# Products of ones in front of waits, and wider moving operands, in a two-layer transformer kernel

## The reference, cut to what matters

```python
def first_block(x, ...):            # attention of three kinds, gated branches
    hn = rms_norm(x, ln_g)
    proj = hn @ w_in                # 1024 x 11520
    # q, k, v, silu gates of: block attention (8 heads), dilated attention (3 x 8 heads),
    # sliding window attention with sinks (8 heads), and sigmoid gates
    merged = sum(sigmoid(gate_i) * ((o_i * silu(g_i)) @ w_branch[i]) for i in range(3))
    return x + merged @ w_out

def hybrid_layer(x, c, ...):
    ada = silu(c) @ w_ada + b_ada   # 1024 x 6144, one row: shifts, scales, gates
    h = rms_norm(x) * (1 + scale1) + shift1
    proj = h @ w_in                 # conv part, q, k, v, index q (512), index k and weights (72 columns)
    # indexed attention: top 64 keys for each query by a relu score, then softmax
    x = x + gate1 * (concat(conv_out, attn_out) @ w_out)
    h2 = rms_norm(x) * (1 + scale2) + shift2
    return x + gate2 * moe(h2, ...) # 64 experts, top 8 of each token, and a shared expert
```

## Time and profile before

| | before |
|---|---|
| median of 3 runs | 1109.86 us (1106.12 to 1110.11) |
| profiled execution | 1112.14 us, span of its instructions 1110.3 us |
| TensorE busy (MATMUL) | 1021.8 us, 92% of the span |
| VectorE, ScalarE, GpSimd busy | 796.2, 585.9, 218.9 us |
| mean granted TensorE clock | 0.950 |
| HBM read | 244.27 MB, 222 GB/s over the span |

### The profile page before, as it was taken

One profiled execution on the slowest core, in us unless ns is written; L12 is line 12 of the kernel. 1 busy time (PEld: TensorE's weight loads), 2 busy tenths in 40 slices (PEclk: granted clock), 3 DMA queues, 4 the chain that ended last, 5 costly groups with the idle time before them and its releaser, 6 DMA issues. The chain is left out here.

```text
span 1110.3 us, 16071 instructions
## 1 busy us (share of the span) xinstructions
PE 1021.8 (92%) x4922; PEld 815.6 (73%) x4922; DVE 796.2 (72%) x1324; ACT 585.9 (53%) x895; POOL 218.9 (20%) x237
## 2 busy tenths in 40 slices
PE   5999999997999998979879697999999999999994
PEld 4878877786766675767668576677888788888883
DVE  4677787676654452556686644789999999999995
ACT  4555555334324432334435331677777777778772
POOL 4032220001000000041140000324324233232330
PEclk9999999997999798988899798999999999999997
DMA  9677676747634224434234213878888888888882
GB/s 321 234 261 247 237 235 227 236 162 235 223 107 171 91 96 170 152 93 157 100 128 152 77 40 116 334 292 334 332 313 343 311 325 340 304 345 331 318 345 79
DMA packets 91204, 247.36 MB, mean 223 GB/s; under 512 B 13244, under 2 KB 23925, under 8 KB 77842
## 3 DMA queue, kind: packets, MB, share of 16 engines
q1 hardware_dynamic: 84578, 226.36, 57.0%
q0 software_dynamic: 6000, 19.96, 4.8%
q10 hardware_dynamic: 576, 0.41, 0.1%
HBM read 244.27 MB, written 2.29 MB: 222 GB/s over the span
## 5 line engine op out<-in xcount | busy, mean ns | idle before, releaser
L1746 PE MATMUL bank<-w_hi,a_hi 128*128 128x512 f32 (+2 forms) x512 | 213.9, 418 | 13.8 <-DVE w_lo L1224 7.1
L1746 PE MATMUL bank<-w_lo,a_hi 128*128 128x512 f32 (+2 forms) x512 | 204.6, 400 | 0.0
L1746 PE MATMUL bank<-w_hi,a_lo 128*128 128x512 f32 (+2 forms) x512 | 204.4, 399 | 0.0
L1224 DVE TENSOR_TENSOR w_lo<-ring,w_hi 128x1024 fp32r<-128x1024 f32 (+2 forms) x134 | 154.4, 1177 | 55.0 <-ACT w_hi L947 51.3
L947 ACT ACTIVATE w_hi<-ring 128x1024 fp32r<-128x1024 f32 (+2 forms) x140 | 141.3, 1024 | 97.9 <-PE bank L1746 94.5
L1614 DVE TENSOR_TENSOR up_lo<-raw_weights,up_hi 128x1024 fp32r<-128x1024 f32 x136 | 164.2, 1247 | 3.0
L1107 ACT ACTIVATE up_hi<-raw_weights 128x1024 fp32r<-128x1024 f32 x136 | 135.8, 1050 | 0.0
L1746 PEld LDWEIGHTS bank<-w_hi,a_hi 128*128 128x128 f32 x512 | 101.9, 199 | 45.7 <-issue 23.2
L793 POOL TENSOR_SCALAR mean_squares<-mean_squares 128x8 f32<-128x8 f32 (+2 forms) x32 | 9.9, 310 | 566.7 <-ACT logits L900 301.8
L1746 PEld LDWEIGHTS bank<-w_hi,a_lo 128*128 128x128 f32 x512 | 101.7, 199 | 21.3
L1746 PEld LDWEIGHTS bank<-w_lo,a_hi 128*128 128x128 f32 x512 | 102.0, 199 | 19.8 <-issue 1.4
(11 more groups left out here) (258 smaller groups left out, 1839.2 us busy)
## 6 DMA issues: line engine op xcount, KB each, us to landing
raw_weights<-in_w_dram SPq DMA_DIRECT2D x102, 1024.0 KB, 7.0
ring<-in_w_in_dram SPq DMA_DIRECT2D x58, 1024.0 KB, 5.3
merged<-in_w_ada_dram SPq DMA_DIRECT2D x96, 256.0 KB, 5.3
ring<-in_w_out_dram SPq DMA_DIRECT2D x8, 1024.0 KB, 5.4
ring<-in_w_branch_dram SPq DMA_DIRECT2D x6, 1024.0 KB, 5.0
bias<-rel_rows SPq DMA_DIRECT2D x40, 128.0 KB, 5.2
block_rows<-place_rows SPq DMA_DIRECT2D x34, 128.0 KB, 8.6
ring<-in_ws_dram SPq DMA_DIRECT2D x2, 1024.0 KB, 4.9
```

Of the source, the lines that this page charges most:

```text
L1224: dve.tensor_tensor(w_parts[1][:, 2 * p:2 * p + 2, 0:w], view(JOB[it[1:3]], kind)[:, 2 * p:2 * p + 2, :], w_parts[0][:, 2 * p:2 * p + 2, 0 ...
L1746: mm = pe.matmul(ps[:, 0:w], a_parts[za][:, k, t * P:(t + 1) * P], w_parts[zw][:, k, 0:w], start=start, stop=stop)
```

## The change

A table KEEP_BUSY gives, for 18 places, a number of products of the 128x128 matrix of ones with itself. `keep_busy` issues them on TensorE in front of the wait of that place, into a bank that is overwritten later. The sixteen at the start run before the wait for the constants. In `ada_out` the eight one-column sums move 64 columns of ones (64 equal columns), and VectorE reads one of each 64. Products of the 72-column chunk move 192 columns; the columns above 72 hold older values and are not read. Two waits (for `probsT` and for `valued`) stand earlier in TensorE's queue than before.

```diff
+KEEP_BUSY = {("start",): 16, ("half", "proj", 2, 0): 9, ("proj", 2, 0): 4, ("flip", 15, 2): 5,
+             ("turn_branch", 2): 6, ("xturn", 1, 0): 4, ("xturn", 1, 1): 15, ("proj2", 0, 0): 4, ("turn2", 0, 3, 0): 7,
+             ("turn2", 1): 10, ("value", 31): 8, ("turn_branch", 3, 1): 17, ("out2", 0, 0): 4, ("route", 0): 4,
+             ("route", 1): 5, ("ranks",): 7, ("tokens", 0): 5, ("last_put",): 22}
...
-                        dve.scalar_tensor_tensor(out=mod[rows, m, :], in0=turn_b[rows, 0:KT], scalar=float(s in (1, 4)),
+                        dve.scalar_tensor_tensor(out=mod[rows, m, :], in0=turn_b[rows, 0:CH:HD], scalar=float(s in (1, 4)),
...
+            begun = 0
+
+            def keep_busy(it, ps=None):
+
+                count = KEEP_BUSY.get(it, 0)
+                if count and ps is None:
+                    ps = use_bank(begun)
+                for _ in range(count):
+                    pe.matmul(ps[:, 0:P], ones[:, :], ones[:, :], start=True, stop=True)
+
             for it in SCHEDULE:
                 kind0 = it[0]
                 if kind0 == "start":
+                    pe.wait_ge(S("ones_set"), 2)
+                    keep_busy(it)
                     pe.wait_ge(S("consts_loaded"), 16)
-                    pe.wait_ge(S("ones_set"), 2)
+                elif kind0 != "route":
+                    keep_busy(it)
...
                     ps = use_bank(n) if begins else proj_b[n % 2]
+                    begun = n + 1
...
-                                    mm = pe.matmul(ps[:, 0:w], a_parts[za][:, k, t * P:(t + 1) * P],
-                                                   w_parts[zw][:, k, 0:w], start=start, stop=stop)
+                                    wide = max(w, 3 * HD)
+                                    mm = pe.matmul(ps[:, 0:wide], a_parts[za][:, k, t * P:(t + 1) * P],
+                                                   w_parts[zw][:, k, 0:wide], start=start, stop=stop)
...
                     for t in range(NT):
+                        keep_busy(it + (t,))
                         turn_bank(TURN[it + (t,)])
...
+                            keep_busy(it + (g, t))
                             wide_bank(TURN[it + (g, t)], 2 * z + t)
...
-                            mm = pe.matmul(turn_b[HD * hf:HD * hf + HD, k:k + 1], acc[:, k:CH:KT], ones[:, 0:1],
+                            mm = pe.matmul(turn_b[HD * hf:HD * hf + HD, HD * k:HD * k + HD], acc[:, k:CH:KT], ones[:, 0:HD],
                                            start=True, stop=True)
...
                         pe.wait_ge(S("probs"), 2 * i + 2)
+                        keep_busy(it + (g,))
...
                 if kind0 == "route":
                     t = it[1]
+                    pe.wait_ge(S("probsT"), len(UNITS))
+                    keep_busy(it, flip_b[1])
...
             job_ready(pe, j)
-            pe.wait_ge(S("probsT"), len(UNITS))
...
+            pe.wait_ge(S("valued"), 64)
+            keep_busy(("ranks",), flip_b[1])
             pe.wait_ge(S("taken_ready"), 2)
-            pe.wait_ge(S("valued"), 64)
...
             pe.wait_ge(S("shared_h_0"), 1)
+            keep_busy(("tokens", 0), hidden_b)
             find_tokens(0, 0)
...
                     with pe.If(n_work > i):
                         expert_block(i, (b + 1) % BODY, m4 + 1 + (b + 2) // BODY)
+            keep_busy(("last_put",), turned_b)
             pe.wait_ge(S("put_ready"), n_work)
```

## The result

| | before | changed |
|---|---|---|
| median (4 runs each, taken side by side) | 1107.99 us (1105.23 to 1110.11) | 1094.99 us (1091.53 to 1097.53) |
| profiled execution | 1112.1 us | 1096.3 us, span 1094.5 |
| TensorE busy | 1021.8 us | 1032.3 us |
| mean granted TensorE clock | 0.950 | 0.978 |

The ratio is 0.9873, with a 95% interval of 0.9839 to 0.9907: faster by 10 to 18 us. The forecast was 1094, from 1082 to 1106. The medians differ by 13.0 us, the two profiled executions by 15.8, because the one of the kernel before lies 4.2 above its median and the one of the changed kernel 1.3 above its own.

What follows compares the result with a forecast made beforehand. TensorE, busy 92% of the span, was taken to set the pace. Gains of 25.3 us less 5.6 at the end and 3.7 for growing waits left 16; from 1112.1, less 2.3 to the median, 1094, range 1082 to 1106.

Steps and rivals of the forecast that it cites:

- a: Start of the kernel: products of ones fill the first waits and raise the clock level early; gain 3.3 us.
- b: Sums of the ada products widened to 64 columns: four lower-level stretches behind them vanish; gain 6.4 us.
- i: Stretch at 623.9, heads 30 and 31 to out2: eight products cost, seventeen fit a wait; gain 1.1 us.
- m: Twenty-two products behind the expert loop, before the last scatter: nothing hides them; loss taken as 5.6 us.
- c: Stretch at 507.8, beginning inside the 72-column products: widening to 192 columns gains 3.2 of up to 4.0 us.
- d: Stretch at 367.9: five products in a wait of 1.51 us in front; gain 3.0 us, half the ceiling.
- e: Stretch at 429.3: six products in a wait of 2.24 us, two unfilled waits following; gain 1.8 us.
- j: Router: four and five products of ones; sixteen router products go from 3.67 to 1.9 us; gain 1.8 us.
- g: Stretch at 531.7, index products with waits between: seven products in turn2; gain 1.3 us.
- All hold: Rival: all fills hold and every lower-level stretch but that at 262.1 goes; 1085 us, chance 12%.
- Hidden anyway: Rival: DMA, ScalarE and VectorE pace the front part, so half the gain passes; 1103 us, chance 12%.
- Fills hold only in part: Rival: fills and wide operands hold the level partly, so stretches move rather than vanish; 1104 us, chance 10%.

Runs made afterwards that it cites:

- five executions: First profile and two unedited repeats of the changed kernel (1098.14, 1096.05 us), plus its versions with none (1090.10) and eleven (1091.04) products behind the expert loop.
- the two repeats: The changed kernel profiled again twice with no edit: 1098.14 and 1096.05 us, one execution each.
- the fastest kernel: Changed kernel without the products behind the loop, before value 31 and the second norm's first transposes; bare waits filled, plus value 30 and flip 18: 1078.97 us.

## Why the prediction was right

The forecast of 1094 held (1095), and most of its steps did. Part of that is luck. The saving was 13.0 us between the medians where 15.9 was forecast, and misses in the parts cancelled.

- **Right in mechanism and size:** a (2.95 for 3.3, of which up to 1.0 is there without products of ones), b (6.1 for 6.4), f, h, k and l, all within 0.4. So is i in this profile (0.79 for 1.1), but over five executions it lies between -0.9 and 0.8, and its range was 0 to 2.3. The 192 columns cost nothing: their step is 0.11 us, as at 72. The wide sums cost 0.07 a group (16 instructions in 2.15 us after, 2.08 before).
- **The end, m, was right.** It was the only large loss, and it was read off the chain as issue time under which nothing can hide. The products took 6.67 against 6.8 to 7.9, the scatter gave 1.66, and taking them out won 4.9. In this profile the term was 0.6 too large because the level came up 3.9 us after they began, at the lower bound of 4 to 6. In the two repeats that took 4.3 and 5.2 us, and the loss was 5.2 and 5.7. In the other kernels it took from 3.3 to 5.9.
- **Failed step, c.** The forecast took 3.2 of 4.0 for the stretch at 507.8 and said in the same sentence what would go wrong: its own idle time of 2.16 gets no fill and can bring the level down again. It did, in every profile that has the 192 columns and leaves that wait bare. The width keeps the level up through those products, but what they save turns into a longer wait for VectorE (from 2.16 to 3.13), so the gain is nil. (In one of the five executions the stretch lasted 3.4 and the part gave 1.4, with nothing changed in it.) The price was put on the cause that the change touches, though a second cause was enough to keep the stretch. Twelve products in that wait gave the 2.6.
- **Failed as well, d: 1.56 for 3.0.** The gain was put down to five products in front of flip 15. The kernel without any gains 1.50 there, so nothing shows that they did anything. The first 6.8 us of the stretch went without them, and no run tells why. The rest stands behind a bare wait of 1.57 us. Six products in that wait, in the fastest kernel, took away the whole stretch and gave 2.3 more (4.14, against 1.85 in the kernel that differs from it up to there by those six alone).
- **Mis-sized the other way: e, 2.9 for 1.8, and j, 2.47 for 1.8.** The waits behind e's fill are 0.7 to 0.9 us, and they left the level up in every profile with this fill but one: the stretch at 415.9 in the fastest kernel (3.4 us) shows that e was not certain. For j only the sixteen router products were counted. The stretch also covered the eight transposes and part of the products behind them. At 675.1 the changed kernel is 3.1 ahead, and 0.6 of that is lost again by 679.6, where the ranks wait for VectorE.
- **Mis-sized: g, 0 for 1.3.** The stretch came again with its full 6.8 us. Over five executions it gave 0, 1.5, 1.5, 1.5 and 3.0, so this term has no single value, and 1.3 was near the middle.
- **The 3.7 for waits that grow** was a judgement, and did not show up as such. In this profile it was used up by c, d and g (5.9 less than forecast), while e, j, k and the loop gave 2.8 more. The total was near because misses cancelled.
- **Rivals.** "All hold" (1085) falls to c, d, g and i. "Hidden anyway" falls at b, where 6.1 of 6.4 arrive, and at e, h, j and k, and holds at 498. "Fills hold only in part" falls because at e, h, j and k the stretches are gone. "Slower" falls because the fills start at the full level in all but three places, the start, the seventeen at 614.17 and the end. The seventeen take 5.15 us and still fit their wait, with 0.28 left. The transposes' rule falls in the run with transposes.

What stays open: what decides in which executions the stretches near 165, 497, 518 and 609 come and for how long, and why d's stretch is shorter without its products. The 0.8 us in the expert loop are no gain of the change that can be shown: without any product of ones the loop gives 1.7, and over the profiled kernels it lies between -0.6 and 1.7. Part of it is TensorE's waits for gathered rows, 1.1 us in the changed kernel, 1.8 before and 2.5 in the kernel with transposes.

## What to carry to other kernels

Work that keeps the clock up belongs in front of the wait, in the instruction order as well as in the trace. Behind the wait, or in issue time, it costs its whole length, so find which semaphore the wait is on before placing it. Look for a bare wait behind each fill before counting its gain: at 498 the stretch stayed until that wait was filled too. Run the kernel without the fills as well, since a gain where one stands need not be its own (d). Profile the same kernel several times before pricing a stretch, since some come by chance.

## What the runs showed of the hardware

- The level fell without any idle time just before it: behind four of the eight groups of one-column sums (16 instructions in 2.08 us), the same four in both kernels that have them, and within the 72-column products (507.8 before, 494.7 in the run with them). With 64 columns (2.15 us) it stayed up in all twelve profiles, and with 192 (0.11 us each, as at 72) it fell only in the wait behind.
- Float32 transposes of 128 x 128 held the level up as products of ones did: 1096.58 against 1094.99 us. At the end of that kernel it rose during a run of nothing but transposes.
- Every stretch at the lower level ahead of the end lasted 3.4, 6.8, 10.2, 13.7 or 17.1 us, in all kernels. Five executions of the same instructions agreed in the stretches near 255 and 364 and differed in four others.
- At the end, after 6.3 us with nothing issued (6.6 in one kernel), the level came back between 3.3 and 5.9 us after work began. For the changed kernel alone it was 3.9, 4.3 and 5.2 in three executions.
